# First condition loaded alone, gate rows a chunk ahead, and a reordered end of each residual update in a three-block fp32 transformer kernel

## Chip, cores and metric

One core of a Trainium2 chip runs the whole program in one launch. The metric is the device time of that launch in microseconds (us). The inputs are fp32 and lie in HBM; the result is 256 tokens of 1024 features.

## What is computed

One sequence of T = 256 tokens, width D = 1024, goes through three blocks, each a mixer and a feed-forward network (FFN). Each of the six halves reads the residual stream x through an RMS norm that a condition vector modulates, and adds its output back through a second RMS norm with a gate from the same vector:

```python
c_act = silu(c)
mod = c_act @ ada_w[layer] + ada_b[layer]           # 1024 x 6144 of weights
sh1, sc1, g1, sh2, sc2, g2 = split(mod, 6)
h = rms_norm(x, g) * (1 + sc1) + sh1
y = mixer(h)                                        # gMLP, then sparse attention, then gated linear attention
x = x + g1 * rms_norm(y, g')
h = rms_norm(x, g'') * (1 + sc2) + sh2
y = ffn(h)                                          # relu(h @ W1)**2 @ W2 twice, then a gated conv FFN
x = x + g2 * rms_norm(y, g''')
```

The attention block reads a second modulated copy of x for its keys and values. The third block has two condition vectors of its own (`c_2` for x, `c_ctx_2` for a context of 256 tokens).

## The kernel before

The kernel is written by hand in one order per engine; engines meet only at counted semaphores. Every engine works strictly in its own order, so an instruction that waits holds up all that stand behind it on its engine.

**Weights.** All weights come through `raw`, a ring of six 1 MB slots that the queue of SyncE (SP) fills in one fixed order. A slot is refilled with load n only when load n - 6 has been used up, and SP does not pass a load that waits. A weight load of kind "M" is split in two: ScalarE (ACT) writes the high part (`hi`, L603) and VectorE (DVE) the rest (`lo`, L1011), which frees the slot. `splits(m)` on either engine does all splits below number m that are still to do. `hi(m)` also waits until the product m - 3 is done, since there are three buffers. TensorE (PE) then multiplies three times per pair of tiles; it waits for `lo(m)` in `split_ready(m)`. A load of kind "A" holds modulation weights. For batches `S0, G0A, S0B, S2, G2B` PE multiplies them as they lie (`ada_chunk`, L1573), for the others DVE accumulates them. When a batch is complete, ACT copies the sums (`ada_row`, L615), PE turns them to columns (`ada_cols`, L1600), and DVE makes the coefficients (`mods`, L1156 and L1145).

**Start.** Five small DMAs on ACT's queue bring the conditions and norm weights as rows (L576); PE transposes all at once, ACT takes `silu`, DVE pads it, and PE does five A chunks, the norm transposes, and three more A chunks, which complete `S0`. SP's queue issues loads 0 to 5 of the ring meanwhile, and x as the third transfer. DVE's split of the first M load (`splits(1)`) stands behind `vectors(1)`. In front of the fourth M load SP issues four row tensors of the gMLP (L548 to L551).

**End of each half.** y (256 x 1024) builds up in PSUM banks 0 to 3. The last product of a half (`rows_onto_y(..., last=True)`, L1725) completes these banks one after the other. The gate's row, spread over all partitions, is `ones @ diag(gate)`: DVE makes the diagonals (`gain_diag`, L1139, tile `tmp`), PE multiplies (`gain_row`, L1607), ACT copies the two halves to `gain` (L621). ACT then squares and sums y bank by bank (`y_squares`, L643). DVE (`update_x`) multiplies y by the gate row (L1105), forms the inverse root (L1072 to L1075, L1107), adds to x (L1113), and makes the diagonal of the next norm (`norm_tile`, tile `xd`, L1084). ACT squares x in between (L655). PE keeps itself busy with 16 idle products (`keep_warm`, L1611), then transposes and norms x in one product (`x_transposes`, L1619). ACT modulates (L675), DVE splits h (`split_h`, L1130 and L1126), and PE starts the next half at the pace of those. There are five such boundaries in the middle and one at the end: after gMLP, FFN 0, attention, FFN 1, the linear attention (GLA), and FFN 2.

The last four products of a mixer that has `w_out` are named `M_AO` (gMLP), `M_BO` (attention) and `M_WO` (GLA). Their numbers are consecutive. In GLA, PE's loop over them stands at L2100 to L2109:

```python
for j in range(4):
    if j == 2:
        pe.wait_ge(s_gs, 1)
    if j == 3:
        gain_row(U_GLA, 0)
        gain_row(U_GLA, 1)
        ada_sum(G2B)
    rows_onto_y(M_WO[j], ...)
    if j == 2:
        ada_chunks(4)
```

ACT has done `splits(M_WO[0] + 3)` at L945 before. In the ring, `M_WO[0..3]` are followed by the four A loads of `G2B`, then by `M_UP[0]` and `M_GA[0]` of the last FFN, so that `M_GA[0]` takes the slot of `M_WO[3]`.

## Time and profile before

| | us |
|---|---|
| median of 3 runs (lowest, highest) | 1176.87 (1176.62, 1178.01) |
| the profiled execution | 1176.72 |
| its span in the trace | 1175.0 |
| PE busy, share of the span | 1095.3, 93% |
| DVE busy | 790.7, 67% |
| ACT busy | 530.5, 45% |
| mean granted TensorE clock | 0.953 |

Busy time of PE includes matmuls that are pipelined, so that it says little by itself; what counts is which wait ends last at each place. "Granted clock" is the share of full TensorE speed that the chip gave (1.00 is 2.4 GHz, 0.50 is 1.2 GHz). Times in the rows are in us from the span's start.

### The profile page before, as it was taken

What the parts mean: (1) busy time and instruction counts of PE and PEld (TensorE: products, weight loads), DVE (VectorE), ACT (ScalarE), POOL (GpSimd) and SP (SyncE); (2) the same over time, 40 slices, a digit from 0 to 9 for tenths busy, and PEclk for the clock granted to TensorE, in tenths of its full rate; (3) what the DMA queues carried; (4) which work ended last, traced back from release to release, by engine and by line L of the source; (5) the groups of instructions that cost most, each with busy time, mean ns of one, the idle gap of its engine ahead of it and who ended that gap; (6) DMA issues with size and microseconds to landing.
All of it is one profiled execution on the core that took longest, in us unless ns stands there. A gap on an engine that the chain in (4) does not pass through costs nothing.

```text
span 1175.0 us, 17657 instructions
## 1 busy us (share of the span) xinstructions
PE 1095.3 (93%) x7315; PEld 945.3 (80%) x7315; DVE 790.7 (67%) x1171; ACT 530.5 (45%) x691; POOL 48.7 (4%) x77
## 2 busy tenths in 40 slices
PE   4999899999998898989899999999997899999997
PEld 1687699888878886877788788889994568999996
DVE  0458598769868754764864579772457568888896
ACT  2441554444454434653535335452732446445443
POOL 0000000000000000000000000040026000000000
PEclk8999999999999986979999999999998799999999
DMA  9996679879948970023575789904440354555610
GB/s 369 312 366 224 242 258 351 322 259 345 329 150 242 336 250 4 2 74 102 187 284 216 285 312 398 346 3 144 144 144 1 108 180 158 197 183 180 204 48 36
DMA packets 129787, 243.59 MB, mean 207 GB/s; under 512 B 6360, under 2 KB 101163, under 8 KB 122539
## 3 DMA queue, kind: packets, MB, share of 16 engines
q1 hardware_dynamic: 125184, 238.76, 57.7%
q10 hardware_dynamic: 4523, 3.70, 1.2%
q8 instruction: 58, 0.95, 0.3%
q14 instruction: 22, 0.18, 0.0%
HBM read 239.30 MB, written 1.05 MB: 205 GB/s over the span
## 4 chain that ended last, share of the span: by engine, by line
PE 76%; DVE 12%; DMA 4%; ACT 3%; issue 2%; POOL 1%; SPq 1%; ACTq 0%; DVEq 0%; POOLq 0%
PE bank L1718 22%; PE bank L1643 11%; PE bank L1645 11%; PE bank L1644 11%; DVE wlo L1011 2%; PE bank L1619 2%; PE bank L1573 2%; DMA raw<-in_ada_w_dram 2%; ACT whi L603 1%; PE bank L1655 1%; DVE x L1113 1%; PE bank L1656 1%; PE bank L1657 1%; PE bank L1906 1%; DMA raw<-in_a_w_in_dram 1%
## 5 line engine op out<-in xcount | busy, mean ns | idle before, releaser
L1011 DVE TENSOR_TENSOR wlo<-raw,whi 128x2048 fp32r<-128x2048 f32 x145 | 328.5, 2272 | 150.6 <-ACT whi L603 149.7
L603 ACT ACTIVATE whi<-raw 128x2048 fp32r<-128x2048 f32 x145 | 274.4, 1896 | 180.2 <-PE bank L1718 62.7
L1643 PE MATMUL bank<-hcat,whi 128*128 128x256 f32 x1096 | 315.2, 288 | 4.8 <-DVE wlo L1011 4.8
L1645 PE MATMUL bank<-hcat,wlo 128*128 128x256 f32 x1096 | 312.2, 285 | 0.0
L1644 PE MATMUL bank<-hcat,whi 128*128 128x256 f32 x1096 | 312.1, 285 | 0.0
L1643 PEld LDWEIGHTS bank<-hcat,whi 128*128 128x128 f32 x1096 | 212.5, 194 | 14.2 <-issue 6.4
L1644 PEld LDWEIGHTS bank<-hcat,whi 128*128 128x128 f32 x1096 | 212.5, 194 | 1.3
L1645 PEld LDWEIGHTS bank<-hcat,wlo 128*128 128x128 f32 x1096 | 212.3, 194 | 0.0
L1531 DVE SCALAR_TENSOR_TENSOR cvt<-ut,vec,cvt 128x189 f32<-128x189 f32 (+2 forms) x176 | 68.2, 429 | 22.7 <-ACT cvt L978 20.3
L1718 PE MATMUL bank<-whi,fhi 128*128 128x512 f32 x240 | 76.9, 401 | 0.0
L1718 PE MATMUL bank<-wlo,fhi 128*128 128x512 f32 x240 | 75.5, 396 | 0.0
L1718 PE MATMUL bank<-whi,flo 128*128 128x512 f32 x240 | 75.4, 395 | 0.0
L1043 DVE SCALAR_TENSOR_TENSOR acc_wide<-raw,csil,acc_wide 128x2048 f32<-128x2048 f32 x28 | 65.6, 2343 | 0.9
L721 ACT ACTIVATE fr<-bank 128x512 f32<-128x512 f32 x32 | 19.1, 598 | 94.9 <-PE bank L1645 88.0
L1718 PEld LDWEIGHTS bank<-wlo,fhi 128*128 128x128 f32 x240 | 45.1, 188 | 10.9
L1718 PEld LDWEIGHTS bank<-whi,flo 128*128 128x128 f32 x240 | 45.1, 188 | 10.9
L1718 PEld LDWEIGHTS bank<-whi,fhi 128*128 128x128 f32 x240 | 43.1, 188 | 13.3 <-issue 5.2
L1243 DVE TENSOR_TENSOR fhi<-fr 128x512 fp32r<-128x512 f32 x32 | 22.1, 690 | 37.7 <-ACT fr L721 37.6
L1718 PE MATMUL bank<-whi,hcat 128*128 128x512 f32 x144 | 41.4, 402 | 1.6 <-DVE hcat L1510 1.3
L1573 PE MATMUL bank<-raw,cpad 128*32 128x512 f32 x256 | 35.2, 658 | 7.1 <-DMA raw<-in_ada_w_dram 6.0
L1619 PEld LDWEIGHTS bank<-xd,x 128*128 128x128 f32 x192 | 27.2, 230 | 17.9 <-DVE xd L1084 16.2
L1619 PE MATMUL bank<-xd,x 128*128 128x128 f32 x192 | 28.3, 316 | 13.7 <-DVE xd L1084 13.7
(376 smaller groups left out, 1793.5 us busy)
## 6 DMA issues: line engine op xcount, KB each, us to landing
raw<-in_ada_w_dram SPq DMA_DIRECT2D x48, 1024.0 KB, 7.6
raw<-in_ff_w_in_dram SPq DMA_DIRECT2D x32, 1024.0 KB, 7.3
raw<-in_ff_w_out_dram SPq DMA_DIRECT2D x32, 1024.0 KB, 7.2
raw<-in_w_ada_dram SPq DMA_DIRECT2D x24, 1024.0 KB, 9.0
raw<-in_w_up_dram SPq DMA_DIRECT2D x22, 1024.0 KB, 5.1
raw<-in_w_in_dram SPq DMA_DIRECT2D x12, 1024.0 KB, 8.1
raw<-in_w_down_dram SPq DMA_DIRECT2D x11, 1024.0 KB, 5.0
raw<-in_a_w_in_dram SPq DMA_DIRECT2D x8, 1024.0 KB, 12.9
```

Of the source, the lines that this page charges most:

```text
L603: act.activation(whi[:, m % SPL, 0:w], raw[:, pl.nm[m] % RAW, 0:w], ACT.Copy).then_inc(s_hi, 1)
L721: act.activation(fr[:, :], ps[pl.bank[u0 + c]][:, :], ACT.Relu).then_inc(s_mid, 1)
L1011: dve.tensor_tensor(wlo[:, m % SPL, 0:w], raw[:, pl.nm[m] % RAW, 0:w], whi[:, m % SPL, 0:w], ALU.subtract).then_inc(s_lo, 1)
L1043: ins = dve.scalar_tensor_tensor(out=to[:, :], in0=w, scalar=s, in1=to[:, :], op0=ALU.mult, op1=ALU.add)
L1243: dve.tensor_tensor(fhi[:, c % 3, :], fr[:, :], fr[:, :], ALU.mult).then_inc(s_fh, 1)
L1531: ins = dve.scalar_tensor_tensor(out=y, in0=grid(ut)[:, frm[0], frm[1]], scalar=vec[:, w_:w_ + 1], in1=y, op0=ALU.mult, op1=ALU.add)
L1573: mm = pe.matmul(ps[ADA_BANK][32 * g:32 * g + 32, :], cpad[:, c, k, :], w, start=i == 0, stop=i == CHUNKS[b] - 1)
L1619: mm = pe.matmul(ps[X_BANKS[kt // 2]][:, c0:c0 + P], x[:, tt, kt * P:kt * P + P], xd[:, tt, :], start=True, stop=True)
L1643: pe.matmul(dst, wh[:, kt, n], ah[:, kt, :], start=kt == 0, stop=False)
L1644: pe.matmul(dst, wh[:, kt, n], al[:, kt, :], start=False, stop=False)
L1645: mm = pe.matmul(dst, wl[:, kt, n], ah[:, kt, :], start=False, stop=kt == KT - 1)
L1718: mm = pe.matmul(y, s, w, start=False, stop=False, skip_group_check=True)
```

## The change

1. **Start.** The row of `c` alone is loaded by SP's queue, ahead of everything; it is transposed, passed through `silu` and padded alone; PE does two A chunks before the other rows. ACT issues the other row loads at once and takes the second `silu` behind them. DVE's first split stands ahead of `vectors(1)`.
2. **gMLP.** ACT copies batch `G0A`'s sums ahead of the wait for the second u product, no longer behind the split of `M_AO[0]`. The sum of `S0B` is copied ahead of two splits.
3. **Gate rows.** In both ReLU FFNs PE multiplies them in chunks 13 and 14 (before: 14 and 15), in gMLP and attention ahead of the third of the last four products (before: the fourth). Banks are chosen for that. In GLA and FFN 2 PE's place for them is not touched.
4. **ACT's splits.** In gMLP, attention and GLA, `splits(M_xO[3])` now stands ahead of the gate rows' copies, and the split of the fourth product behind them.
5. **`update_x`.** DVE adds each half of the first token tile as soon as it can, and sums the statistics of the second in between; `mods` goes behind the norm's diagonals.
6. **Boundary.** 22 idle products in place of 16, behind a wait for the half's gate rows.
7. The context's DMA (L880) goes behind the first epilogue of FFN 1.

The new semaphores and blank lines are left out:

```diff
@@ -17,7 +17,7 @@
-WARM_LEVEL, WARM_BOUNDARY, WARM_START = 3, 16, 3
+WARM_LEVEL, WARM_BOUNDARY, WARM_START = 3, 22, 3
@@ -472,7 +473,7 @@
-    GAIN_BANKS = {U_GMLP: (4, 5), U_FF0: (4, 4), U_ATT: (4, 5), U_FF1: (4, 4), U_GLA: (4, 5), U_FF2: (7, 5)}
+    GAIN_BANKS = {U_GMLP: (5, 6), U_FF0: (6, 4), U_ATT: (7, 6), U_FF1: (6, 4), U_GLA: (4, 5), U_FF2: (7, 5)}
@@ -541,6 +542,7 @@
+            sp.dma_start(vrow[0:8, 0, :], v8(I["c"][0])).then_inc(s_c8, 16)
@@ -571,11 +573,11 @@
-            for row, src in ((0, v8(I["c"][0])), (8, v8(I["c_2"][0])), (16, v8(I["c_ctx_2"])),
+            for row, src in ((8, v8(I["c_2"][0])), (16, v8(I["c_ctx_2"])),
...
                 act.dma_start(vrow[row:row + src.shape[0], 0, :], src).then_inc(s_crow, 16)
-            act.wait_ge(s_vec, 1)
-            act.activation(csil[:, :], vec[:, 0:24], ACT.Silu).then_inc(s_sg, 1)
+            act.wait_ge(s_c8v, 1)
+            act.activation(csil[:, 0:8], vec[:, 0:8], ACT.Silu).then_inc(s_sg, 1)
@@ -593,6 +595,9 @@
+            act.wait_ge(s_vec, 1)
+            act.activation(csil[:, 8:24], vec[:, 8:24], ACT.Silu).then_inc(s_sg, 1)
@@ -691,6 +696,8 @@
                     m = M_U[j]
+                    if j == 1:
+                        ada_row(G0A)
@@ -698,14 +705,13 @@
                         act.activation(lr[:, 1, :], lr[:, 0, :], ACT.Sqrt).then_inc(s_lr, 1)
-                    if j == 1:
-                        ada_row(G0A)
-                splits(M_AO[3] + 1)
                 use_roots()
+                splits(M_AO[3])
...
                 gain_row(U_GMLP, 1)
+                splits(M_AO[3] + 1)
+                ada_row(S0B)
                 splits(M_AO[3] + 3)
-                ada_row(S0B)
@@ -726,9 +732,9 @@
                     epi(c)
-                    if c == 15:
-                        gain_row(u, 0)
-                    splits(m0 + 2 * c + 4)
+                    if c >= 14:
+                        gain_row(u, c - 14)
+                    splits(m0 + min(2 * c + 4, 33))
@@ -739,6 +745,8 @@
                         act.dma_start(b2v[:, :], I["cmp_b2"][1:2].broadcast_to([P, HD])).then_inc(s_aw, 16)
+                    if c == 0 and f == 1 and has("gla"):
+                        act.dma_start(ctx_tm[:, :, :], I["ctx_2"][0].rearrange("(t p) d -> p t d", p=P)).then_inc(s_ctx, 16)
@@ -751,7 +759,7 @@
                         act.activation(root[:, :], sv[:, 0, :], ACT.Sqrt).then_inc(s_root, 1)
-                gain_row(u, 1)
+                splits(m0 + 34)
@@ -866,7 +874,7 @@
                 high(NPAIR - 1)
-                splits(M_BO[3] + 1)
+                splits(M_BO[3])
@@ -876,8 +884,6 @@
                 splits(M_FF[1] + 3)
-                if has("gla"):
-                    act.dma_start(ctx_tm[:, :, :], I["ctx_2"][0].rearrange("(t p) d -> p t d", p=P)).then_inc(s_ctx, 16)
@@ -955,10 +961,12 @@
                 use_roots()
-                splits(M_WO[3] + 3)
+                splits(M_WO[3])
...
                 gain_row(U_GLA, 1)
+                splits(M_WO[3] + 1)
                 ada_row(G2B)
+                splits(M_WO[3] + 3)
@@ -1092,32 +1100,50 @@
-            def update_x(u, e=None, between=None):
-                dve.wait_ge(s_gain, 2 * u + 2)
...
+            def update_x(u, e=None, later=None):
+                def times_gain(i):
+                    dve.wait_ge(s_sqy, 4 * u + i + 1)
+                    n = slice(512 * (i % 2), 512 * (i % 2) + 512)
+                    dve.tensor_tensor(yg[:, i // 2, n], ps[i][:, :], gain[:, n], ALU.mult).then_inc(s_yg, 1)
+                def half_of_y(tt):
+                    dve.wait_ge(s_sqy, 4 * u + 2 * tt + 1)
+                    first_half(ssy, tt)
+                def norm_of_y(tt):
+                    dve.wait_ge(s_sqy, 4 * u + 2 * tt + 2)
...
                     link(dve.tensor_tensor(rsy[:, tt:tt + 1], r, q, ALU.mult))
-                    if tt and e is not None:
-                        half_of_x(e, 0)
...
-                if between is not None:
-                    mods(between)
+                def add(i):
+                    dve.wait_ge(s_yg, 4 * u + i + 1)
+                    tt, n = i // 2, slice(512 * (i % 2), 512 * (i % 2) + 512)
+                    dve.scalar_tensor_tensor(out=x[:, tt, n], in0=yg[:, tt, n], scalar=rsy[:, tt:tt + 1], in1=x[:, tt, n],
+                                             op0=ALU.mult, op1=ALU.add).then_inc(s_x, 1)
+                dve.wait_ge(s_gain, 2 * u + 2)
+                half_of_y(0)
+                times_gain(0)
+                times_gain(1)
+                norm_of_y(0)
+                add(0)
+                half_of_y(1)
+                add(1)
+                times_gain(2)
+                times_gain(3)
+                norm_of_y(1)
+                if e is not None:
+                    half_of_x(e, 0)
+                add(2)
+                add(3)
...
                     norm_tile(e, 1)
+                if later is not None:
+                    mods(later)
@@ -1163,9 +1189,12 @@
                 dve.wait_ge(s_vT, n + 1)
-                dve.tensor_copy(vec[:, V0[i]:V0[i + 1]], ps[2 + n % 2][:, 0:NV[i]]).then_inc(s_vec, 1)
-            vectors(0)
+                r = 0 if n else 8
+                dve.tensor_copy(vec[:, V0[i] + r:V0[i + 1]], ps[2 + n % 2][:, r:NV[i]]).then_inc(s_vec, 1)
+            dve.wait_ge(s_c8T, 1)
+            dve.tensor_copy(vec[:, 0:8], ps[2][:, 0:8]).then_inc(s_c8v, 1)
@@ -1173,12 +1202,14 @@
             dve.tensor_copy(cpad[:, 0, :, 0], csil[:, 0:8]).then_inc(s_cp, 1)
+            vectors(0)
+            dve.wait_ge(s_sg, 2)
...
             norm_x(0)
+            splits(1)
...
             dve.wait_ge(s_vec, 2)
-            splits(1)
@@ -1621,6 +1652,13 @@
+            def boundary(e):
+                pe.wait_ge(s_gain, 2 * e)
+                keep_warm(WARM_BOUNDARY, 6)
+                x_transposes(e)
@@ -1742,21 +1780,21 @@
-                keep_warm(WARM_BOUNDARY, 6)
-                x_transposes(2 * f + 1)
+                boundary(2 * f + 1)
...
                 for c in range(16):
+                    if c == 14:
+                        pe.wait_ge(s_gain, 2 * u + 1)
...
                         ada_sum(ends_at(f, c - 1))
-                    if c == 14:
-                        pe.wait_ge(s_mid, u0 + 14)
-                        gain_row(u, 0)
-                    if c == 15:
-                        gain_row(u, 1)
+                    if 13 <= c < 15:
+                        pe.wait_ge(s_mid, u0 + c)
+                        gain_row(u, c - 13)
@@ -1769,12 +1807,15 @@
             pe.wait_ge(s_const, 5)
-            pe.wait_ge(s_crow, 16 * 5)
-            vectors(0)
-            pe.wait_ge(s_cp, 3)
+            pe.wait_ge(s_c8, 16)
+            pe.transpose(ps[2][:, 0:8], vrow[0:8, 0, :], ident[0:8, 0:8]).then_inc(s_c8T, 1)
+            pe.wait_ge(s_cp, 1)
...
             pe.wait_ge(s_cpad0, 2)
-            ada_chunks(5)
+            ada_chunks(2)
+            pe.wait_ge(s_crow, 16 * 4)
+            vectors(0)
+            ada_chunks(3)
@@ -1826,7 +1867,7 @@
                         mix(3)
-                    if j == 3:
+                    if j == 2:
@@ -1838,8 +1879,7 @@
             if has("attn"):
-                keep_warm(WARM_BOUNDARY, 6)
-                x_transposes(2)
+                boundary(2)
@@ -1975,7 +2015,7 @@
                     pe.wait_ge(s_oh, 2 * j + 2)
-                    if j == 3:
+                    if j == 2:
@@ -1984,8 +2024,7 @@
             if has("gla"):
-                keep_warm(WARM_BOUNDARY, 6)
-                x_transposes(4)
+                boundary(4)
@@ -2110,8 +2149,7 @@
             if has("ffn2"):
-                keep_warm(WARM_BOUNDARY, 6)
-                x_transposes(5)
+                boundary(5)
```

## Rows read from the trace of the kernel before

**Rows 1.** The page: the chain that ended last, by engine.
```profile
PE 76%; DVE 12%; DMA 4%; ACT 3%; issue 2%; POOL 1%; SPq 1%; ACTq 0%; DVEq 0%; POOLq 0%
```

**Rows 2.** Chain of waits, 0 to 60 us (start, us, what).
```profile
4.17 18.95 DMA raw<-in_ada_w_dram
...
43.09 13.00 DMA raw<-in_a_w_in_dram
```

**Rows 3.** Timeline of the start (start, us, engine line op; idle before, releaser).
```profile
0.80 0.86 SPq L541 DMA_DIRECT2D raw<-in_ada_w_dram  x2
...
20.65 1.91 ACT L603 ACTIVATE whi<-raw 128x2048 fp32r<-128x2048 f32 x1 [0.55 <-DMA raw<-in_a_w_in_dram]
...
23.16 1.94 PE L1573 MATMUL bank<-raw,cpad 128*32 128x512 f32 x8 [5.46 <-DMA raw<-in_ada_w_dram]
...
32.87 2.29 DVE L1011 TENSOR_TENSOR wlo<-raw,whi 128x2048 fp32r<-128x2048 f32 x1
```

**Rows 4.** Timeline of PE in gMLP.
```profile
60.41 0.38 PE L1655 MATMUL bank<-whi,hcat 128*128 128x256 f32 x1 [1.52 <-DVE wlo L1011]
...
89.00 1.05 PE L1600 MATMUL bank<-sel,stage 128*128 128x2 f32 x8 [2.06 <-ACT stage L615]
```

**Rows 5.** Timeline, boundary after gMLP.
```profile
126.62 1.88 PE L1607 MATMUL bank<-tmp,one 128*128 128x512 f32 x4
...
129.03 3.71 ACT L603 ACTIVATE whi<-raw 128x2048 fp32r<-128x2048 f32 x2
...
133.11 0.60 ACT L643 ACTIVATE t<-bank 128x512 f32<-128x512 f32 x1
...
134.64 3.61 PE L1611 MATMUL bank<-zb 128*128 128x512 bf16 x16
...
142.64 5.39 PE L1619 MATMUL bank<-xd,x 128*128 128x128 f32 x32 [4.39 <-DVE xd L1084]
```

**Rows 6.** Timeline of PE, boundary after FFN 0.
```profile
340.47 3.61 PE L1611 MATMUL bank<-zb 128*128 128x512 bf16 x16
345.74 3.84 PE L1619 MATMUL bank<-xd,x 128*128 128x128 f32 x32 [1.66 <-DVE xd L1084]
```

**Rows 7.** Timeline of ACT, boundary after attention.
```profile
553.64 0.59 ACT L643 ACTIVATE t<-bank 128x512 f32<-128x512 f32 x1
```

**Rows 8.** Timeline of PE, boundary after attention.
```profile
547.62 1.88 PE L1607 MATMUL bank<-tmp,one 128*128 128x512 f32 x4
...
562.75 5.26 PE L1619 MATMUL bank<-xd,x 128*128 128x128 f32 x32 [4.30 <-DVE xd L1084]
```

**Rows 9.** Timeline of PE, boundary after FFN 1.
```profile
773.89 5.47 PE L1619 MATMUL bank<-xd,x 128*128 128x128 f32 x32 [2.09 <-DVE xd L1084]
```

**Rows 10.** Timeline of DVE, the same boundary.
```profile
778.70 0.88 DVE L1130 CAST hcat<-t 128x256 fp32r<-128x256 f32 x2 [2.96 <-ACT t L675]
...
782.02 0.28 DVE L1130 CAST hcat<-t 128x256 fp32r<-128x256 f32 x1
```

**Rows 11.** Timeline of GpSimd (POOL), the same boundary.
```profile
779.36 1.73 POOL L2207 TENSOR_SCALAR_AFFINE_SELECT lmask<-lmask 128x128 int8<-128x128 int8 x1
```

**Rows 12.** PE by windows: us, busy, granted clock, DMA share, GB/s.
```profile
142.60:148.00 5.40, 5.36 (x33) 0.69 0.00 0
```

**Rows 13.** Timeline of ACT, end of GLA.
```profile
957.87 1.91 ACT L603 ACTIVATE whi<-raw 128x2048 fp32r<-128x2048 f32 x1 [7.74 <-DMA raw<-in_w_up_dram]
...
960.75 0.60 ACT L621 ACTIVATE gain<-bank 128x512 f32<-128x512 f32 x1 [0.26 <-PE bank L1607]
```

**Rows 14.** Timeline of DVE, end of GLA.
```profile
950.47 4.49 DVE L1011 TENSOR_TENSOR wlo<-raw,whi 128x2048 fp32r<-128x2048 f32 x2
```

**Rows 15.** Timeline of PE, end of GLA.
```profile
958.73 1.98 PE L1607 MATMUL bank<-tmp,one 128*128 128x512 f32 x4
...
971.77 3.84 PE L1619 MATMUL bank<-xd,x 128*128 128x128 f32 x32 [1.31 <-DVE xd L1084]
```

**Rows 16.** DMA issues by line, whole span (KB each, median us to landing).
```profile
raw<-in_w_up_dram SPq DMA_DIRECT2D x22, 1024.0 KB, 5.1
```

More of the change, by code:

```diff
@@ L1093, in norm_x @@
                     norm_tile(e, tt)
-            def update_x(u, e=None, between=None):
-                dve.wait_ge(s_gain, 2 * u + 2)
-                for tt in range(2):
-                    for half in range(2):
-                        dve.wait_ge(s_sqy, 4 * u + 2 * tt + half + 1)
-                        if half == 0:
-                            first_half(ssy, tt)
-                        n = slice(512 * half, 512 * half + 512)
-                        dve.tensor_tensor(yg[:, tt, n], ps[2 * tt + half][:, :], gain[:, n], ALU.mult).then_inc(s_yg, 1)
+            def update_x(u, e=None, later=None):
[8 more added lines that the diff above has]
+                    dve.wait_ge(s_sqy, 4 * u + 2 * tt + 2)
@@ L1106, in update_x @@
                     r, q = rsqrt(ssy, tt)
                     link(dve.tensor_tensor(rsy[:, tt:tt + 1], r, q, ALU.mult))
-                    if tt and e is not None:
-                        half_of_x(e, 0)
-                    for half in range(2):
-                        dve.wait_ge(s_yg, 4 * u + 2 * tt + half + 1)
-                        n = slice(512 * half, 512 * half + 512)
-                        dve.scalar_tensor_tensor(out=x[:, tt, n], in0=yg[:, tt, n], scalar=rsy[:, tt:tt + 1], in1=x[:, tt, n],
-                                                 op0=ALU.mult, op1=ALU.add).then_inc(s_x, 1)
```

3 lines of the change are left out of this document (2 added, 1 removed).

## The prediction, on record before the changed kernel was seen

> **What bounds the kernel.** I read the page first: PE holds 76% of the chain that ended last, DVE 12% and DMA 4% [rows 1]. Work beside PE's steady stream costs nothing; what counts are the places where PE stands still. I looked for these in the chain of waits and then in PE's timeline, for idle time with a releaser. The chain names two DMAs at the start [rows 2]: one modulation load, 18.95 us from issue to landing, which releases PE at 23.16 after 5.46 us of idleness [rows 3], and a gMLP load issued at 43.09. Then come PE waits of 1.52 and 2.06 us in gMLP [rows 4], and the five boundaries, where PE waits 4.39, 1.66, 4.30, 2.09 and 1.31 us for the norm's diagonal, after its idle products [rows 5, 6, 8, 9, 15]. After the waits of 4.39, 4.30 and 2.09 the same 32 matmul records take 5.39, 5.26 and 5.47 us; after 1.66 and 1.31 they take 3.84. The windows say why: the granted clock of the first case is 0.69 [rows 12], so part of it ran at 1.2 GHz. Over 5.40 us that is 1.67 us lost, and 5.39 less 3.84 is 1.55: the short ones ran at 2.4 GHz.
>
> **Start: +0.4.** The row of c is a new issue ahead of the ring's first load. SP takes 0.43 us for an issue (0.86 for two [rows 3]), and the load for which PE waits until 23.16 was issued at 4.17 [rows 2] as the last of a backlog: all of it starts 0.4 later. The bounds are 0, if the queue has slack, and 0.9, twice the issue. That PE does two A chunks some microseconds earlier buys nothing, because the fifth chunk still waits for that load and the rest up to `S0` is serial on PE. It does free slots earlier, but the loads that get them come behind the one that matters, and these transfers land in order: the M load issued just ahead of it reached ACT at 20.65, it reached PE at 23.16 [rows 3]. The Trainium skill ("DMA: Bandwidth & Descriptors", section on queues, rings and completion order) says that an engine consumes one ring's descriptors in ring order; the trace agrees, with 2.5 us between the two landings, and by that rule the sum stays as it is.
>
> **gMLP: -1.5 and -2.1.** DVE's first split ran at 32.87, behind `vectors(1)` [rows 3], although ACT's part was done at 22.6 (20.65 + 1.91). It frees a slot, and SP stands in front of that slot. Done at about 23 to 25, it lets three loads go during 25 to 31, and the four row tensors and the fourth M load follow some 5.5 us earlier than 43.09 [rows 2]. PE waited 1.52 us for that load's split [rows 4]; PE was busy up to there, so that 1.52 is all that there is to gain. At 89.00 PE waited 2.06 us for ACT's copy of `G0A`'s sums [rows 4], which stood behind the split of `M_AO[0]`, itself held up by a DMA until 86.55. The copy now waits for neither. DVE's coefficients follow the columns, and its layer norm and the mixing follow them serially, so the 2.06 goes through. Sum with the start: -3.2; I say -3.1.
>
> **Boundary after gMLP: -3.0 and -1.5.** The gate rows cost PE 1.9 us in either place. Before, they were followed on ACT by two splits (3.71 us from 129.03) and a copy, so the squares began at 133.11, although the first bank was complete a quarter into the product that started at 128.5 [rows 5]. Now the gate rows are done before the third product: ACT copies them by 123.5, splits the fourth product until 125.4, DVE until 127.7; PE needs it at 128.5 (126.62 + 1.88). Of the two splits left, the second waits for the third product's end at 128.5 and ends at 130.45. Squares start 2.65 earlier. From the first square DVE works back to back up to the diagonal (9.53 us; 0.39 of that was `mods`, which goes behind). So the transposes start at 142.64 - 2.65 - 0.39 = 139.6. 22 idle products of 0.226 us (3.61 / 16) last from 134.64 to 139.6: no gap, so the clock stays, and the transposes take 3.84 instead of 5.39: -1.5.
>
> **After FFN 0: -0.3.** The squares already follow the banks, and DVE has the same instructions in another order, back to back. Only the `mods` in front of the diagonal goes (0.39), and the 22 products end at 345.44, so PE starts 0.3 earlier than 345.74 [rows 6]. Its clock was full before.
>
> **After attention: -2.2 and -1.4.** As after gMLP, without `mods`: the third product now starts at 544.0 and ends at 549.5 (547.62 + 1.88 [rows 8]), ACT's second split follows it until 551.45, against squares at 553.64 [rows 7]. Transposes at 560.6 against 562.75, idle under 1 us, full clock: 5.26 becomes 3.84.
>
> **After FFN 1: -1.2.** The diagonal comes 0.39 earlier and the transposes run 1.6 us faster [rows 9], but then DVE meets POOL's masks, which start with the end of FFN 1 and last until 781.1 whatever DVE does [rows 11]. Two casts take 0.88 us there, one takes 0.28 afterwards [rows 10]. The bounds are 0.4 (only the diagonal) and 2.0 (all of it). At about half speed until 781.1, DVE has some 1.1 us more work behind it by then than before. I take 1.2 of the 2.0. The Trainium skill ("GPSIMD Engine Reference", specifications) has POOL's SBUF interfaces shared with VectorE, in contention with two-input instructions or those in a two-port mode; that agrees with the slow rows.
>
> **End of GLA: +9.9 and +1.5.** Here ACT's order changes and PE's does not. `splits(M_WO[3])` does nothing, since `splits(M_WO[0] + 3)` has done as much before. The split of the fourth product, which DVE did in the first half of its stretch from 950.47 [rows 14] and ACT before it, now stands behind ACT's copies of the gate rows, which PE makes directly in front of that very product at 958.73 [rows 15]. ACT's second copy ends at 961.3 [rows 13]; ACT's split lasts until 963.2 (1.91), DVE's until 965.5 (2.25, half of 4.49), so PE starts the product at 965.5 and not at 960.7: 4.85 us idle. And the slot: `M_GA[0]`'s load waits for `M_WO[3]`'s low part, which is now over at 965.5, not 952.8 (950.47 + 2.25). Landing takes 5.1 us [rows 16]: 970.6. ACT splits it ahead of the squares (before: at 957.87, as soon as it had landed [rows 13]), until 972.5. The product itself ends at 971.1, or 972.7 with a fallen clock, so the squares start at 972.5. Then DVE's 9.11 us as after attention (553.64 to 562.75 [rows 7, 8]): transposes at 981.65 against 971.77 [rows 15], +9.9. The idle products end at 978.4 at the latest, so PE waits some 3.3 us; waits of 2.09 to 4.39 were followed by the lower clock: +1.5.
>
> **The rest: 0.** At the very end DVE's work is the same in sum and the last output waits for the last add. In FFNs PE's gate rows only change place; the diagonals are ready over 9 us before. ACT's extra 0.6 us there is covered by PE's next 5.6 us product. The context's DMA is needed several chunks later.
>
> Sum: -3.1 - 4.5 - 0.3 - 3.6 - 1.2 + 11.4 = -1.3. The profiled execution took 1176.72 (span 1175.0), 0.15 below the median 1176.87. So 1175.4.
>
> **Rivals.**
> - *The GLA stall doesn't spread.* If the load of `M_GA[0]` lands before the squares need ACT, only the stall counts: product ends 972.7, idle products until 978.4, transposes then, +6.6 for +11.4, and 1170.6. For it: before, that load's split was off the path. Against: the slot rule is in SP's code.
> - *No stall in GLA at all*, since some of ACT's order is covered: 1175.4 - 11.4 = 1164.0. Only a misreading of the orders gives this; the numbers of the products are consecutive.
> - *The clock falls all the same* (the other side). If the 22 idle products don't hold it through the transposes, the 1.5, 1.4 and, of the 1.2, 0.9 are missing: 1179.2, slower. It decides once PE's granted clock in two of the three is under 0.8. For it: idle products ran before too, and 2.09 us of waiting behind them was enough. Against: 1.66 and 1.31 did no harm, and the waits now are under 1 us.
> - *The start brings nothing*: the load issued at 43.09 took 13.00 us [rows 2], so DMA was backed up there, and if the earlier issues only queue, -1.5 becomes 0 and the 0.4 stays: 1176.9.
>
> **Chances.** As summed 0.58 (own range 1173.0 to 1178.0, from half a microsecond on each of six terms and one on the GLA chain), stall alone 0.12, no stall 0.04, clock 0.16, start 0.10. The range takes in the stall-alone case and the clock case: 1170.0 to 1180.0. What a measurement of this kernel can tell from no change is 0.2%, 2.35 us: faster is below 1174.5. The first two special cases and 0.2 of the summed one are faster: 0.36. The clock case and a little of the others are slower: 0.14. Same: 0.50.
>
> **What would show it.** Right: PE's wait at the fourth M load and at `G0A` gone; squares of gMLP starting some 2.6 us before their old distance from the end of the last product; transposes of 3.84 us with granted clock 1.00 at the first four boundaries; in GLA a PE wait of about 4.9 us for DVE's `wlo` in front of L1725 and ACT's `whi` waiting for a `w_up` DMA behind it, PE idle about 3 us before the fifth transposes. Wrong: a fourth product of gMLP or attention that waits for its split (margins are 0.8 and 0.5 us); transposes still above 5 us; no wait in GLA.

## The result and the profile after

The changed kernel takes 1179.18 us (median of 20, 1177.58 to 1181.5), the kernel before 1177.46 beside it: a ratio of 1.002, 95% interval 1.001 to 1.0029. It is 1.7 us slower, where 1.3 less were forecast. The profiled execution took 1180.70 (span 1179.0), 3.98 more than the profiled one of before. All times in rows are us from the span's start.

PE's timeline after, at the start and at the first four boundaries:

```profile
23.28 1.94 PE L1604 MATMUL bank<-raw,cpad 128*32 128x512 f32 x8 [3.94 <-DMA raw<-in_ada_w_dram]
...
39.04 0.36 PE L1706 MATMUL bank<-whi,hcat 128*128 128x256 f32 x1 [1.62 <-DVE hcat L1156]
...
133.29 4.91 PE L1642 MATMUL bank<-zb 128*128 128x512 bf16 x22
138.23 3.84 PE L1650 MATMUL bank<-xd,x 128*128 128x128 f32 x32
...
339.49 3.84 PE L1650 MATMUL bank<-xd,x 128*128 128x128 f32 x32
...
556.89 3.84 PE L1650 MATMUL bank<-xd,x 128*128 128x128 f32 x32 [1.09 <-DVE xd L1092]
...
766.23 3.84 PE L1650 MATMUL bank<-xd,x 128*128 128x128 f32 x32 [0.42 <-DVE xd L1092]
```

These answer to [rows 3, 5, 6, 8, 9]. The fifth A chunk comes 0.12 us later than before, the first product of gMLP (L1706) 1.54 later (before 37.50). From there on the changed kernel catches up: the transposes stand at -4.41, -6.25, -5.86 and -7.66 us against before, and all four take 3.84. The two waits of [rows 4] are gone. Between 47.2 and 340 us PE stands still for over 0.2 us only in front of the mixing (1.13 us, at 97.61) and for a low part (0.58 us, at 112.24).

The end of GLA, first on PE, then on ACT, then in the chain that ended last:

```profile
957.86 0.80 PE L1763 MATMUL bank<-whi,hcat 128*128 128x512 f32 x1 [4.81 <-DVE wlo L1019]
...
965.82 4.91 PE L1642 MATMUL bank<-zb 128*128 128x512 bf16 x22
974.23 5.47 PE L1650 MATMUL bank<-xd,x 128*128 128x128 f32 x32 [3.49 <-DVE xd L1092]
```

```profile
963.03 1.92 ACT L608 ACTIVATE whi<-raw 128x2048 fp32r<-128x2048 f32 x1 [5.26 <-DMA raw<-in_w_up_dram]
964.85 0.57 ACT L648 ACTIVATE t<-bank 128x512 f32<-128x512 f32 x1
```

```profile
953.58 1.91 ACT whi L608
955.51 2.30 DVE wlo L1019
957.83 5.17 DMA raw<-in_w_up_dram
963.03 1.92 ACT whi L608
964.94 0.58 ACT t L648 x2
```

Read from the top, the chain is the forecast one: high part, low part, the load that waits for the slot, its high part, the squares. Before, the transposes stood at 971.77 [rows 15]; a lead of 7.66 has become a lag of 2.46. With 5.47 for 3.84 us and what follows, the lag at the next PE wait is 3.99: the end of GLA costs 11.65 us, 11.4 were forecast.

### The profile page after: what moved, and what is told of

It reads as the page before. It is cut to its first block, busy times and chain, and to the rows that moved or that the text cites. A ratio compares the mean times of both kernels' runs of the same rounds, so it can differ in the third digit from the quotient of the medians.

```text
span 1179.0 us, 17733 instructions
## 1 busy us (share of the span) xinstructions
PE 1105.2 (94%) x7346; PEld 949.2 (81%) x7346; DVE 792.0 (67%) x1172; ACT 531.1 (45%) x692; POOL 49.3 (4%) x77
## 4 chain that ended last, share of the span: by engine, by line
PE 80%; DVE 10%; ACT 3%; issue 2%; DMA 2%; POOL 1%; SPq 0%; ACTq 0%; DVEq 0%; POOLq 0%
PE bank L1756 21%; PE bank L1681 12%; PE bank L1683 11%; PE bank L1682 11%; DVE wlo L1019 2%; PE bank L1604 2%; PE bank L1650 2%; PE bank L1693 2%; PE bank L1695 2%; PE bank L1694 2%; DMA raw<-in_ada_w_dram 2%; ACT whi L608 1%; PE bank L1946 1%; PE bank L1968 1%; PE bank L1638 1%
## 5 line engine op out<-in xcount | busy, mean ns | idle before, releaser
L680 ACT ACTIVATE t<-bank,mod,coef 128x256 f32<-128x256 f32 x64 | 30.4, 583 | 17.8 <-PE bank L1650 12.5
L1642 PE MATMUL bank<-zb 128*128 128x512 bf16 x143 | 35.9, 398 | 0.0
```

The costliest lines, as they stand in the source:

```text
L680: act.activation(t32[:, kt, :], ps[banks[kt // 2]][:, T * (kt % 2):T * (kt % 2) + T], ACT.Identity, scale=coef[:, c, kt:kt + 1], bias=mod[ ...
L1642: pe.matmul(ps[bank][:, :], zb[:, 0:P], zb[:, :], start=True, stop=True)
```

## The experiments

Each was timed beside the kernel before, whose median was 1177.28 beside runs 1 to 4, 1177.72 beside 5 to 8, 1177.14 beside 9 to 11 and 1177.11 beside 12 to 14. "Less" and "more" below are differences of medians. The interval of a ratio is 0.2 to 0.4% to either side, 2 to 4 us, so that sizes of about 1 us rest on the traces and not on the medians.

**1. GLA's order of before**, in the changed kernel.

```diff
                 use_roots()
-                splits(M_WO[3])
+                splits(M_WO[3] + 3)
                 gain_row(U_GLA, 0)
                 gain_row(U_GLA, 1)
-                splits(M_WO[3] + 1)
                 ada_row(G2B)
-                splits(M_WO[3] + 3)
                 y_squares(U_GLA, M_WO[3])
```

> The changed kernel with ACT's order at the end of GLA as before: all splits of the last four products ahead of the gate rows' copies. In the changed kernel the stall of the fourth product (4.81 us) and the waits that follow it made the end of GLA 11.6 us dearer than before, with the lower clock in the transposes. Theory (the order is the whole cost, stall and cascade): no wait at the fourth product, transposes at full clock, end of GLA back to its old length, 11.5 us less than the changed kernel: about 1167.7 against 1179.2, 0.8% faster than the kernel before. Rival (only the stall of 4.8 us is due to the order, the rest to the changed update of x): 1174.4. Rival (the work of PE and DVE in the last FFN takes up the difference): under 3 us gained.

1167.38 us, ratio 0.9928 (0.9907 to 0.995): 11.8 less than the changed kernel. PE stands still nowhere from the first of the four products to the end of the transposes, which take 3.84 us. The order is the whole cost, and all the rest of the change together gives 9.9 us.

**2. The same order put into the kernel before** (the diff the other way round).

> The kernel before with nothing but ACT's new order at the end of GLA: M_WO[3]'s split behind the gate rows' copies, M_GA[0]'s split ahead of the squares. Theory (the order costs by itself what the two traces show): 1177.5 + 11.5 = 1189.0, with a PE wait of about 4.8 us for DVE's low part at the fourth product and the squares 10 us later than before. Rival (it costs only together with the new update of x and the longer idle products): 1177.5 + 4.8 = 1182.3. Rival (the load of M_GA[0] has slack here): squares start right behind the product, 1182.3 also, but without ACT waiting for a w_up transfer.

1189.47 us, 12.2 more than before, ratio 1.0115 (1.0079 to 1.0152). PE's timeline shows the same wait, to the hundredth, in a kernel that has nothing else of the change:

```profile
970.05 0.79 PE L1727 MATMUL bank<-whi,hcat 128*128 128x512 f32 x1 [4.81 <-DVE wlo L1013]
```

**3. The stall without the load behind it.** In the changed kernel:

```diff
                 ada_row(G2B)
-                splits(M_WO[3] + 3)
+                splits(M_WO[3] + 2)
                 y_squares(U_GLA, M_WO[3])
+                splits(M_WO[3] + 3)
```

> The changed kernel, but the split of M_GA[0] at the end of GLA stands behind the squares of y and no longer ahead of them; the split of the fourth product stays behind the gate rows' copies. It takes away the cascade and leaves the stall. Theory of the prediction (stall 4.8 us; the rest is that the squares wait on ACT behind the landing of M_GA[0], and the fall of the clock behind the longer wait): the fourth product still waits 4.8 us, squares follow its banks, transposes at 3.84 us; 4.8 to 6.8 us less than the changed kernel, 1172.4 to 1174.4. Rival (the cascade is not on the path: the landing is the same and the first product of the last FFN waits for that split instead): no more than 1 us less, with a PE wait for wlo in the first or second product of the last FFN.

1174.79 us, ratio 0.9993 (0.9972 to 1.0014), 4.4 less than the changed kernel and 7.4 more than run 1. The wait of 4.81 is there, the squares follow their banks, the transposes take 3.84 behind 0.58 of idleness, and no split is late behind them. So the 11.8 are 7.4 for the stall and 4.4 for the landing of `M_GA[0]` in front of the squares. The 7.4 are more than the wait of 4.81, because the fourth product behind it lasts 7.69 us (959.66 to 967.35) where it lasts 5.89 in run 1 (952.35 to 958.24). The expectation's range ended 0.4 short.

**4. The row of `c` with the others again**, in run 1's kernel: `c` goes back into ACT's list of rows, PE transposes all rows at once and does five A chunks in a block. DVE's early split stays.

> The changed kernel with two parts undone: GLA's order as before, and the row of c loaded and transposed with the other rows again, so that PE does five A chunks in one block (DVE's early split stays). Theory (the start lost about 2.6 us, since A chunks that come one at a time as their loads land leave PE at its lower clock for the transposes and the first product of gMLP): 2.6 us less than the run with GLA's order alone, about 1165.1; granted clock in 40 to 45 us back at 1.00, first product of gMLP at 37.5 and done 1.5 us sooner than 39.04 says. Rival (the start's loss is the delay of SP's loads, 0.4 us as predicted): 0.1 to 0.4 us less, about 1167.4. Rival (the start's loss is taken up by the wait at the fourth M load, which comes back): equal within 0.2 us.

1167.45 us, ratio 0.9925 (0.9901 to 0.9949), 0.07 more than run 1, timed beside it. The trace has the first product of gMLP at 37.54, 1.33 before run 1's 38.87, and the medians show no such difference. So I looked at the kernels that start as before does. Their first products come at 37.50 (before), 37.90 (run 2), 38.12 (run 5) and 37.86 (run 12), and their waits for the fourth M load are 1.52, 0.35, 0.59 and 0.54. The profile of before that I had was the quickest start of the four, and it has by far the longest wait. Run 6, which starts as this run does, with the early split, has its first product at 38.31, 0.77 after this run's. So one trace can be off by 0.6 to 0.8 us at this point.

**5. 35 idle products at each boundary of the kernel before.**

```diff
-WARM_LEVEL, WARM_BOUNDARY, WARM_START = 3, 16, 3
+WARM_LEVEL, WARM_BOUNDARY, WARM_START = 3, 35, 3
```

> The kernel before with one constant changed: 35 idle products at each boundary in place of 16 (7.9 us, about as long as 3.61 us plus the longest wait, 4.39). Theory (the long waits behind the idle products are what lets the clock fall, and a PE that doesn't stand still keeps it): transposes of 3.84 us at all five boundaries, so 1.55, 1.4 and 1.6 us less at the three where they took 5.39, 5.26 and 5.47; the idle products outlast the diagonal by nothing after gMLP and attention, by 2.6 after FFN 0, 2.2 after FFN 1 and 3.0 after GLA. Sum: 4.6 less, 7.8 more, about 3 us slower than before, with the transposes at 3.84. Rival (idle products don't hold the clock, only the earlier diagonal did in the changed kernel): transposes stay above 5 us, 8 us slower.

1180.3 us, ratio 1.0027 (1.0007 to 1.0048), 2.6 more; 3 were expected. PE's timeline after gMLP and after FFN 1:

```profile
136.40 7.71 PE L1611 MATMUL bank<-zb 128*128 128x512 bf16 x35
144.41 3.84 PE L1619 MATMUL bank<-xd,x 128*128 128x128 f32 x32 [0.29 <-DVE xd L1084]
...
771.77 7.71 PE L1611 MATMUL bank<-zb 128*128 128x512 bf16 x35
```

The transposes are those of before, with the diagonals of before, and take 3.84 where they took 5.39, 5.26 and 5.47. It is the standing still in front of them that costs the clock.

**6. The two gMLP parts alone**, in the kernel before.

```diff
                     m = M_U[j]
+                    if j == 1:
+                        ada_row(G0A)
                     act.wait_ge(s_mm, m + 1)
...
-                    if j == 1:
-                        ada_row(G0A)
...
             norm_x(0)
+            splits(1)
             vectors(1)
             dve.wait_ge(s_vec, 2)
-            splits(1)
```

> The kernel before with two parts of the change alone: DVE's first split ahead of the second transposed rows, and ACT's copy of batch G0A's sums ahead of the wait for the second u product. Prediction's steps: the waits of 1.52 us at the fourth M load and of 2.06 us for the copy are gone, 3.6 us less than before, 1173.9. Rival (the earlier loads only queue): the wait at the fourth M load stays, 2.1 less, 1175.4. Rival (the time goes into the next wait: DVE's coefficients, layer norm or the mixing's transposed weights end last): equal to before within 1 us, with a new PE wait between 89 and 100 us.

1175.14 us, 2.6 less, ratio 0.9985 (0.9969 to 1.0002): the interval holds the expected 3.6 and also no gain at all. Both waits are gone. The wait for the fourth M load, 1.52 us in the profile that I read, is 0.35 to 0.59 in three others, and the one for `G0A` is 2.46, 1.90 and 1.36 there (runs 2, 5 and 12). A new wait stands in front of the mixing:

```profile
96.80 2.92 PE L1813 MATMUL bank<-wT,v_tm 128*128 128x128 f32 x24 [1.13 <-issue]
```

Before and runs 2 and 5 have no such wait, run 12 has one of 1.12. What differs is the clock behind the wait for `G0A`: after 2.06, 2.46 and 1.90 us the records of the next product lie 0.21 us apart for some 3 to 5 us, after 1.36 (run 12) or no wait (run 6) 0.12 throughout. The mixing starts 9.79 and 9.90 us after the columns in runs 6 and 12, which is the pace of DVE's layer norm, and 10.19, 11.53 and 11.75 us after them in before and runs 2 and 5, where PE itself is late. So the third rival of the expectation is right in that a new wait appears, but it gives back no more than PE's lead over DVE; the lower clock behind the old wait had cost 0.4 to 2 us that the prediction did not count.

**7. Eight idle products in front of the fifth A chunk**, in run 1's kernel.

```diff
             vectors(0)
-            ada_chunks(3)
+            ada_chunks(2)
+            keep_warm(8, 6)
+            ada_chunks(1)
```

> The changed kernel with GLA's order of before, and 8 idle products between the fourth and fifth A chunk, where PE waits 3.7 us for the load. Theory (A chunks that come one at a time as loads land leave PE at the lower clock for the next 20 us; with work in the gap the clock is up when the fifth chunk and the transposes come): transposes at 4.4 us or less against 5.8, first product of gMLP at 6.0 us against 7.5, together 2.5 us less than the same kernel without them in the trace, and about 1165 against 1167.4 in time. Rival (in the timed runs the start isn't on the path, as undoing the start's change moved the median by 0.07 us): the trace's start is shorter, the median is the same within 0.5. Rival (one gap is not enough): neither changes.

1164.92 us, ratio 0.9895 (0.9862 to 0.9929). The trace does what was expected: PE's windows give a granted clock of 1.00 for 40 to 45 us, where the changed kernel has 0.69, and the first product comes at 36.78. But run 14 below leaves the same eight out of run 13's kernel, and the median is lower without them. The gain in the trace is shown, one in the time is not.

**8. Idle products in three waits of attention**, in run 1's kernel: 10 ahead of `M_KW`, 19 ahead of `M_Q[2]`, 12 ahead of the first scores, each in a bank that is free.

> The changed kernel with GLA's order of before, and idle products in three waits of attention: 10 ahead of the fourth key product (wait 2.67 us), 19 ahead of the third query product (4.59 us) and 12 ahead of the first scores (3.12 us). In the trace the records behind these waits are twice as far apart (granted clock 0.50 to 0.75 in 401 to 416 us, 0.50 in 445 to 457). Theory (standing still lets the clock fall, and that is what the changed kernel lost in attention, 2.1 us of its 6.3 us lead, and more that both kernels lose): granted clock 1.00 from 360 to 440, 3 to 5 us less than without, about 1163. Rival (the lower clock there comes from light work of the products ahead, not from the waits): the records keep their spacing, 1167.4. Rival (the waits end later when PE is faster, since DVE's splits of the weights set the pace): clock 1.00 but the waits grow by as much, 1167.4.

1173.81 us, ratio 0.997 (0.995 to 0.9991), 6.4 more than run 1, timed apart. It was none of the three theories: two of my places were wrong. PE's timeline:

```profile
408.28 0.55 PE L1679 MATMUL bank<-hcat,whi 128*128 128x256 f32 x1 [4.68 <-DVE wlo L1017]
...
415.82 4.27 PE L1640 MATMUL bank<-zb 128*128 128x512 bf16 x19
```

The product that waits is `M_Q[1]`; the 19 stand one product later, where nothing waits, and take their 4.27 us. The scores wait behind their first pair, not ahead of it, and the 12 take 3.51 us at 440.25. In the trace the second scores come 3.0 us later than in run 1's (449.42 against 446.44), and the whole takes 3.0 us more; what the medians have beyond that is not explained. A row's line number is that of the helper; which use of it waits has to be counted out.

**9. GpSimd's masks held back** until DVE has split GLA's h, in run 7's kernel (`pool.wait_ge(s_h, 8 * 6)` ahead of the triangles). The trace of the changed kernel had DVE and GpSimd like this:

```profile
772.56 1.74 DVE L1156 CAST hcat<-t 128x256 fp32r<-128x256 f32 x1
774.22 0.40 DVE L1152 TENSOR_TENSOR hcat<-t,hcat 128x256 fp32r<-128x256 f32 x1
774.54 0.28 DVE L1156 CAST hcat<-t 128x256 fp32r<-128x256 f32 x1
```

```profile
770.41 1.75 POOL L2243 TENSOR_SCALAR_AFFINE_SELECT lmask<-lmask 128x128 int8<-128x128 int8 x1
...
772.29 1.86 POOL L2245 TENSOR_SCALAR_AFFINE_SELECT lmask<-lmask 128x128 int8<-128x128 int8 x1
```

> The run with idle products at the start, and GpSimd's triangles and masks of GLA held back until DVE has split GLA's h. In the changed kernel PE's transposes after FFN 1 came 7.66 us ahead of before, with 3.84 us in place of 5.47, and yet the next milestone is ahead by the same 7.66: 1.6 us got lost between them. Theory (DVE's casts run at a third of their speed while GpSimd makes the masks, until a time that doesn't move with DVE): the casts take 0.28 us each at once, first product of GLA 1 to 1.6 us sooner after the transposes, 1.2 to 1.6 us less than 1164.9. Rival (ACT's modulation sets the pace there, not DVE): the casts are short and PE's milestone stays. Rival (the masks are now late): a new PE or DVE wait for GpSimd behind 785 us, time equal or longer.

1167.94 us, ratio 0.9932 (0.9906 to 0.9957), 3.0 more than run 7, timed apart. Every cast of GLA's h takes 0.28, as expected, and PE's wait of 1.0 us for the split is gone. But the masks now meet DVE's next splits of weights, and PE waits for those:

```profile
784.57 0.39 PE L1691 MATMUL bank<-whi,hcat 128*128 128x256 f32 x1 [1.62 <-DVE wlo L1017]
```

From the transposes to the last four products of GLA run 9's trace takes 0.5 us more than run 7's; the rest of the 2.3 us between the two traces was there before the masks, in attention. So the masks do take DVE's time, and moving them by these few microseconds only moves who pays.

**10. The right query product**, in run 7's kernel: 14 zero products of 256 columns added onto the open bank ahead of the fourth compress product, and 19 idle ones ahead of `M_Q[1]`.

```diff
                         m = M_CW[j][c]
+                        if j and c:
+                            for _ in range(14):
+                                pe.matmul(ps[j][:, 0:T], zb[:, 0:P], zb[:, 0:T], start=False, stop=False)
                         split_ready(m)
...
-                linear_mid(M_Q[1], hh, hl)
+                linear_mid(M_Q[1], hh, hl, warm=19)
```

> The run with idle products at the start, and 14 zero products of 256 columns ahead of the fourth compress product (wait 1.79 us for DVE's low part) and 19 idle ones of 512 ahead of the second query product (wait 4.59). In the attempt before, the 19 stood ahead of the third query product, which doesn't wait, and so cost 4.3 us. Theory (standing still at 398 and 404 to 409 us lets the clock fall; what follows at half speed until 415 costs 2 to 3 us): granted clock 1.00 from 395 to 430, 2 to 3 us less at the scores, 1162.5 against 1164.9. Rival (the clock falls at 401 whatever PE does): idle products at half speed take 8 us where PE would wait 4.6, 2 to 4 us more. Rival (DVE's splits pace this stretch): clock 1.00, time within 0.5 of 1164.9.

1156.57 us, ratio 0.9839 (0.9811 to 0.9868): 8.4 less than run 7, timed apart (7.8 when each is set against the kernel before beside it). PE's timeline there:

```profile
397.69 0.39 PE L1906 MATMUL bank<-whi,bw 128*128 128x256 f32 x1 [0.24 <-DVE wlo L1017]
400.65 4.28 PE L1640 MATMUL bank<-zb 128*128 128x512 bf16 x19
405.40 0.39 PE L1679 MATMUL bank<-hcat,whi 128*128 128x256 f32 x1 [0.47 <-DVE wlo L1017]
```

The granted clock is 1.00 from 395 to 430 us; run 7's trace has 0.50 for 405 to 410. The scores come 4.1 us sooner than in run 7, against 2 to 3 expected, and the stretch from the first turn of the heads to the second's values takes 8.4 us where run 7 takes 13.2, because the clock is up there too. Run 12 shows that this stretch can take 8.4 us without any filling, so part of the gain may be that the quicker kind of execution became the usual one: five of the six took 1155.1 to 1156.9, one 1163.8.

**11. 16 idle products instead of 22**, in run 1's kernel.

> The changed kernel with GLA's order of before and 16 idle products at each boundary, not 22. PE then waits 1.4 us longer for the diagonal: about 1.4 after gMLP, 1.1 after FFN 0, 2.5 after attention and 1.8 after FFN 1. Theory (waits of 2.09 us and more behind the idle products were followed by the lower clock, 1.66 and less were not): the transposes after attention take 5.3 us, after FFN 1 perhaps, the others 3.84: 1.4 to 2 us more than 1167.4. Rival (the earlier diagonals alone hold the clock, the 6 more idle products do nothing): 1167.4 within 0.5.

1168.56 us, ratio 0.9937 (0.9912 to 0.9961), 1.2 more than run 1, timed apart and within the intervals; the trace decides. PE's timeline after attention and after FFN 1 (the first row ends at the window's edge; the whole takes 5.47):

```profile
556.69 3.54 PE L1648 MATMUL bank<-xd,x 128*128 128x128 f32 x21 [2.39 <-DVE xd L1090]
...
767.39 3.84 PE L1648 MATMUL bank<-xd,x 128*128 128x128 f32 x32 [1.71 <-DVE xd L1090]
```

2.39 us of waiting lost the clock; 1.71 here, and 1.32, 1.41 and 1.32 at the other three, did not.

**12. The boundaries alone**: the changed kernel with GLA's order, the start and both gMLP parts as before.

> The changed kernel with GLA's order, the start and both gMLP parts as before: what is left are the gate rows, ACT's splits in gMLP and attention, the new update of x, the later coefficients and 22 idle products. Prediction's steps for these: 4.5 + 0.3 + 3.6 + 1.2 = 9.6 us less than before, 1167.7 against 1177.3. By the traces of the changed kernel: 4.4 + 0.3 + 3.1 + 0.4 = 8.2 less, 1169.1. Rival (the parts are not additive: with the waits of 1.5 and 2.1 us of gMLP back, all three together give what they gave one by one, 9.9 less 2.6): 7.3 less, 1170.0.

1169.78 us, ratio 0.993 (0.9905 to 0.9955): 7.3 less than before, which is what additivity asks, 9.9 less 2.6. That it fits to the tenth is luck, with an interval of 2.9 us to either side. Two of its seven executions took 1164.1 and 1164.3 us, the others 1169.2 to 1172.5, and the profiled one is of the two. PE's windows for 455 to 465 us, before and in this run:

```profile
455.00:465.00 10.00, 8.84 (x45) 0.50 0.00 0
```

```profile
455.00:465.00 10.00, 9.23 (x87) 1.00 0.01 2
```

At these first heads of attention the same code runs at 1.2 GHz in one trace and at 2.4 in the other; from the first turn to the second's values it is 13.2 us in the one and 8.4 in the other, 4.8 apart. Within one program only times and mean clocks are on record: the two short executions of run 12 have a mean granted clock of 0.963 and 0.961, its others 0.953 to 0.957. The kernel before beside it has two such executions, 1170.5 and 1171.9 us at 0.961 and 0.959, where the others take 1176.6 to 1179.3 at 0.949 to 0.954. That these, too, gain their time at the first heads is likely and not shown.

**13 and 14. Two more waits of attention**, in run 10's kernel: 12 idle products behind the first scores, 10 ahead of the values of head 12. Run 14 leaves out the eight of the start.

```diff
                 pe.wait_ge(s_gt, 1)
+                keep_warm(12, 4)
...
                     turn(2 * p + 1)
+                    if p == 6:
+                        pe.wait_ge(s_Tev, 28)
+                        keep_warm(10, 4)
                     values(2 * p)
```

> The run with idle products at the start and ahead of the second query product, with two more places in attention: 12 idle products behind the first scores, where PE then waits 3.12 us, and 10 ahead of the values of head 12, where it waits 3.23; from there the trace shows a granted clock of 0.50 for 17 us. Theory (standing still lets the clock fall): the clock stays at 1.00 there, 2 to 3 us less from the half-speed products behind, 1154 against 1156.6; not more, since the heads go at the pace of ACT. Rival (idle products end later than the waits or their bank holds up the next turn): 1 to 3 us more. Rival (the fall there comes from the light work ahead): clock 0.50 as before, 1156.6.

> The same kernel without the 8 idle products between the fourth and fifth A chunk, on the same chip. Theory (they hold the clock up for the transposes and the first product; the trace had 2.1 to 2.5 us): 2 to 2.5 us more than with them. Rival (undoing the start's change moved nothing in time, so the start's speed is lost again at the fourth M load): equal within 0.5.

Run 13: 1156.86 us (1151.08 to 1157.99, four executions), ratio 0.9818 (0.9789 to 0.9847). Run 14: 1153.37 (1152.39 to 1161.38, six executions), ratio 0.981 (0.978 to 0.9839), 23.7 us less than before and the lowest median of all. Its windows, PE:

```profile
440.00:450.00 10.00, 8.49 (x74) 1.00 0.01 2
450.00:460.00 10.00, 9.22 (x85) 1.00 0.00 0
460.00:470.00 10.00, 8.66 (x78) 1.00 0.01 3
500.00:510.00 10.00, 9.33 (x83) 1.00 0.32 107
510.00:520.00 10.00, 9.95 (x46) 1.00 0.33 107
```

Before has 0.67, 0.50, 0.66, 1.00 and 0.56 in the same windows. The expectation's 2 to 3 us for the two waits are within what the medians of runs 10, 13 and 14 leave open (0.3 more to 3.2 less). Whether the start's eight idle products are worth anything stays open: the two traces are 2.3 us apart in their favour, and the medians 3.5 apart against them.

## Why the prediction was wrong

| step | forecast | by medians | by the two profiles |
|---|---|---|---|
| start, row of `c` | +0.4 | 0 (run 4 against run 1) | +1.54 |
| gMLP, two waits | -3.5 | -2.6 (run 6 against before) | -3.12 |
| boundaries | -9.6 | -7.3 (run 12 against before) | -8.37 |
| attention's body | 0 | in the -7.3 | +2.29 |
| end of GLA | +11.4 | +11.8 (changed against run 1), +12.2 (run 2 against before) | +11.65 |
| sum | -1.3 | +1.9; the kernel itself +1.7 | +3.99 |

The last column is how the distance between the two traces changes over each stretch. It is read on PE at the first product of gMLP, at the mixing, behind each set of transposes and at the first wait of FFN 2, and for the end of attention's body at DVE's low part of the last heads (533.36 for 537.32). The mechanisms were the forecast ones, and the parts add up within the intervals. What failed is sizes of the gains, by 3.2 us in all by the medians: the gMLP waits, the step after FFN 1, and attention's body, which the sum put at nothing without a word. The 0.4 for the start, which did not show in time, and the 0.4 that GLA's loss was short of cancel. The measured 1179.18 is almost the 1179.2 of the rival in which the clock falls all the same; that is coincidence, since the traces rule this rival out. It also lies outside the 1173.0 to 1178.0 given for the sum.

- **Start, not settled.** The load came 0.12 us later, the first product 1.54: the transposes of x took 5.86 us where before's profile has 4.51. Other kernels that start as before does take 5.16 to 5.43 there, and run 4, with the rows together, is no faster in time.
- **gMLP, 0.9 too much by the medians, within the interval.** The step "PE was busy up to there, so that 1.52 is all that there is to gain" took the wait from one execution. It depends on how quick the start was; three other traces have 0.35 to 0.59. The other wait's 2.06 went through, as forecast, with the lower clock behind it on top (run 6).
- **After gMLP and FFN 0: right.** From the mixing to open banks the lead grows by 4.40, forecast 4.5; after FFN 0 by 0.27, forecast 0.3. Idle products with no gap, or a gap of 1.09 at most, kept the full clock, as runs 5 and 11 confirm from both sides. The rival "the clock falls all the same" is out.
- **After attention, 0.3 too much.** Set against DVE's low part of the last heads, the squares start 2.16 earlier (547.52 for 553.64), as forecast, and the diagonal 1.90: in its new order DVE's work up to the diagonal takes 8.19 us and not 7.94. The step "from the first square DVE works back to back" left out a gap of 0.30 ahead of its first multiplication. The clock gave its 1.4.
- **After FFN 1, 0.8 too much.** The lower bound was right: 0.38. The transposes' 1.6 us went to DVE, whose cast beside the masks took 1.74 at its worst. I had reckoned with half speed, from one row of two casts in 0.88; the earlier DVE met GpSimd where a single one takes twice that. Run 9 shows the cause: without the masks beside them the casts take 0.28 each and PE's wait of 1.0 us is gone.
- **Attention's body, 1.3 us that no step had.** From `M_KW`'s product to the second scores the trace has 82.55 us in the changed kernel and 81.94 to 83.41 in runs 1, 3, 4, 7, 9, 11 and 12, where attention's waits are not filled; the average of the eight is 82.56. Before has 80.42, runs 2, 5 and 6 have 81.98, 81.82 and 80.68; the average of these four is 81.23. Most of it is one place. The clock falls at 401 us in the changed kernel, behind a wait of 1.79 us, and in before, behind the same wait of 1.79, only in the next one of 4.59. The way from the one product that waits to the next is 9.0 us in the changed kernel, 8.9 to 9.2 in runs 1, 3, 4, 9, 11 and 12, and 7.7 in before and runs 2, 5 and 6, but also in run 7, which differs from run 1 by eight idle products at the start. So the cause is not settled, and neither is whether it is the change at all; run 10 shows that with both waits filled the clock doesn't fall.
- **GLA, right.** 4.81 against 4.85 for the stall, the landing at 963.0 (970.6 less the lead of 7.66 is 962.9), transposes 10.1 us late against 9.9, 5.47 for 3.84. The price of the rival "the stall doesn't spread" was fair too: 4.8 under the sum, and run 3, which builds it, is 4.4 under the changed kernel.

By the medians the change costs 0.15%, inside the 0.2% that the prediction called no change; the side of the forecast, faster, is what the interval of 1.001 to 1.0029 rules out.

## What to carry to other kernels

Before a split, a copy or any work is moved behind another on an in-order engine, ask whose slot it frees: here one moved split cost 7.4 us as a stall and 4.4 through the load that waited for the slot. A wait of an otherwise steady PE can cost twice, once in itself and once in the half-speed work behind it, as the stall of 4.81 us did; idle products pay where the wait is certain and ends after them, and cost their full length one product further. And a term of 1 or 2 us read from one profiled execution should be checked against a second one before it is put into a sum.

## What the hardware showed

- The same 32 products take 3.84 us or 5.3 to 5.5 (6.79 in run 2, behind 4.40), depending on how long PE stood still before: 1.09, 1.32, 1.41, 1.66 and 1.71 us kept the clock, 2.09, 2.39, 3.49, 4.30 and 4.39 lost it. Behind the columns in gMLP 1.36 us kept it and 1.90, 2.06 and 2.46 lost it. But ahead of the query product the clock fell behind 1.79 in some kernels and not in others, and ahead of the fourth key product 2.63, 2.72, 2.70 and 2.72 us kept it at 1.00 (runs 4, 7, 13 and 14) where 2.61 and 2.68 lost it (changed kernel, before). So the length of the wait does not decide alone, and this list is no rule for a place with other work around it.
- The same start gives other times in other executions: the first product of gMLP at 37.50 to 38.12 us in four kernels that are alike up to there, and at 37.54 and 38.31 in two others that are alike. The Trainium skill ("TensorE: Matmul & The Clock Gate", section "What's actually happening") says that the number of slow matmuls at the start of one and the same kernel varies between runs. These traces agree: the 32 transposes of x take 4.51, 5.21, 5.43 and 5.16 us in before and runs 2, 5 and 12.
- Eight A-chunk matmul records take 1.94 us in each of the changed kernel's five loads that land one by one, behind waits of 0.72 to 3.94 us, and 1.07 us with idle products in front (run 7, fifth chunk). In before the fifth chunk's 1.94 us have a granted clock of 0.50, which is 1.2 GHz. For the changed kernel's chunks the level is read from the length alone; its windows give 1.00 there.
- In attention the first heads ran at a granted clock of 0.50 in before's trace and of 1.00 in run 12's, over 10 us and with the same code there; that is 4.8 us of its time. Executions of one program fall into two such groups, some 5 to 7 us apart, the shorter at a mean granted clock about 0.008 higher (run 12 and the kernel before beside it).
